# Writing out PE's four loops in a hybrid decoder step (GLA, short convolution, PEER experts)

## What is computed

```python
h = rmsnorm(x, norm1_g)
p = h @ w_in                                   # 2048 -> 16400
q, k, v, r, alr, cb, cc, cx, ga, gb = split(p)
loga = log_sigmoid(alr @ w_alpha_up + b_alpha) / 16
o, s_gla_new = gla_chunked(q, k, v, loga, s_gla)       # 4 heads, 256 x 512 states
y_a = silu(r) * rmsnorm(o, gla_norm_g)
u = cc * cx;  z = conv_b + sum_j buf[:, j:j+L] * conv_w[j]   # width 3
y_b = cb * z
m = sigmoid(ga) * y_a + sigmoid(gb) * y_b
x = x + m @ w_out
x = x + peer(rmsnorm(x, norm2_g), w_query, sub_keys, expert_u, expert_v)
y = rmsnorm(x, norm_f_g)
```

## Time and profile before

| what | value |
|---|---|
| median of 3 runs | 2507.85 us (2504.65 to 2508.5) |
| the profiled execution | 2509.17 us, of which its span is 2506.9 us |
| mean granted TensorE clock | 0.856 |
| PE busy | 1855.8 us (74%), 9451 matmuls |
| DVE busy | 1654.6 us (66%) |
| POOL busy | 967.6 us (39%) |
| ACT busy | 633.3 us (25%) |
| PE busy from 255 to 417 us (first head) | 160.92 of 162 us |
| PE busy from 601 to 767 us (third head) | 165.11 of 166 us |
| DMA share from 1240 to 2507 us (experts) | 1.00, 416 GB/s |

### The profile page before, as it was taken

The page is one execution under the profiler, slowest core; times in us unless marked ns, Lnnn a source line. Parts: engine busy times, 40 slices in busy tenths (PEclk is TensorE's granted clock), DMA queues, the critical chain, the costliest instruction groups (busy, mean ns, idle before and its releaser), DMA issues.

```text
span 2506.9 us, 26095 instructions
## 1 busy us (share of the span) xinstructions
PE 1855.8 (74%) x9451; PEld 1298.4 (52%) x9451; DVE 1654.6 (66%) x2086; ACT 633.3 (25%) x876; POOL 967.6 (39%) x761
## 2 busy tenths in 40 slices
PE   7999999999999998863655665665555456666564
PEld 6999888889888888852323332322212122122221
DVE  4444454545545545467687887788988887678776
ACT  5433554544545543321110011100101010010000
POOL 0000211111111100024476665666766656567653
PEclk9999999999999999976787887877787767976777
DMA  6665776776776766448899999999999999999997
GB/s 176 174 176 155 222 219 197 219 207 190 224 205 202 224 189 178 123 152 310 335 424 413 414 415 414 426 427 426 410 426 426 427 426 427 426 414 413 426 427 316
DMA packets 424229, 777.17 MB, mean 310 GB/s; under 512 B 14040, under 2 KB 344144, under 8 KB 355464
## 3 DMA queue, kind: packets, MB, share of 16 engines
q0 software_dynamic: 89168, 597.86, 57.8%
q1 hardware_dynamic: 333792, 175.71, 25.5%
q10 hardware_dynamic: 1168, 2.18, 0.2%
HBM read 754.51 MB, written 21.25 MB: 309 GB/s over the span
## 4 chain that ended last, share of the span: by engine, by line
DMA 29%; PE 15%; POOL 7%; DVE 6%; issue 3%; another core or an unknown queue 1%; ACT 1%; ACTq 0%; DVEq 0%; SPq 0%; POOLq 0%
DMA ring<-in_expert_v,idx_all 21%; PE bank L1643 8%; POOL ring L635 7%; DMA raw<-in_w_query 3%; DMA ring<-in_expert_u,idx_all 3%; DVE ring L1294 2%; PE bank L1489 2%; PE bank L1490 1%; PE bank L1491 1%; DVE x_tok L1312 1%; DMA ring<-in_expert_v,idx_s 1%; PE bank L1632 1%; PE bank L1633 1%; PE bank L1634 1%
## 5 line engine op out<-in xcount | busy, mean ns | idle before, releaser
L1643 PE MATMUL bank<-ring,diag 128*128 128x512 f32 x1000 | 672.7, 835 | 497.9 <-DMA ring<-in_expert_v,idx_all 421.4
L1643 PEld LDWEIGHTS bank<-ring,diag 128*128 128x128 f32 x1000 | 260.2, 273 | 899.4 <-issue 816.2
L1294 DVE CUSTOM_DVE_ANT_0 ring<-ring,xn_tok 128x2048 f32<-128x2048 f32 x256 | 583.4, 2289 | 200.1 <-DMA ring<-in_expert_u,idx_all 196.5
L1489 PE MATMUL bank<-act_hi,w_hi 128*128 128x264 f32 x2352 | 686.1, 292 | 17.7 <-DVE act_lo L1157 8.0
L1490 PE MATMUL bank<-act_lo,w_hi 128*128 128x264 f32 x2352 | 673.0, 286 | 0.0
L1491 PE MATMUL bank<-act_hi,w_lo 128*128 128x264 f32 x2352 | 672.0, 286 | 0.0
L964 DVE TENSOR_TENSOR w_lo<-raw,w_hi 128x2048 fp32r<-128x2048 f32 x147 | 337.0, 2292 | 428.6 <-ACT w_hi L665 428.3
L635 POOL DMA_INDIRECT ring<-in_expert_u,idx_all x256 | 443.0, 1730 | 265.4 <-DVE w_all L1294 131.6
L635 POOL DMA_INDIRECT ring<-in_expert_v,idx_all x256 | 391.0, 1527 | 256.8 <-PE bank L1643 182.6
L1489 PEld LDWEIGHTS bank<-act_hi,w_hi 128*128 128x128 f32 x2352 | 449.2, 191 | 76.9 <-issue 68.5
L665 ACT ACTIVATE w_hi<-raw 128x2048 fp32r<-128x2048 f32 x161 | 307.8, 1913 | 648.0 <-PE bank L1491 497.7
(11 more groups left out here) (231 smaller groups left out, 1321.3 us busy)
## 6 DMA issues: line engine op xcount, KB each, us to landing
raw<-in_w_in SPq DMA_DIRECT2D x129, 1024.0 KB, 6.3
s_ring<-in_state_gla POOLq DMA_DIRECT2D x64, 256.0 KB, 5.3
out<-s_ring POOLq DMA_DIRECT2D x64, 256.0 KB, 5.5
raw<-in_w_out SPq DMA_DIRECT2D x16, 1024.0 KB, 5.9
raw<-in_w_query SPq DMA_DIRECT2D x16, 1024.0 KB, 34.3
v_row<-v_samples POOLq DMA_DIRECT2D x32, 256.0 KB, 5.0
ring<-in_expert_u,idx_all POOLq DMA_INDIRECT x256, 14.0
ring<-in_expert_v,idx_all POOLq DMA_INDIRECT x256, 14.7
```

The lines of the kernel that those rows point to most:

```text
L1294: v.tensor_tensor_reduce(ring[k][:], ring[k][:], xn_tok[:, b // PH, :], 1.0, 0.0, ALU.mult, ALU.add, w_all[:, b * TOPK + s:b * TOPK + s + ...
L1489: mm(out, hi_, act_hi[:, k, :], start=(k == 0), stop=False)
L1643: ins = mm(bank[sum_bank(t) + j][:], diag[nth % N_DIAG][:], ring[k][:, j * 512:(j + 1) * 512], start=first, stop=final)
```

## The change

PE's four loops become Python loops, so that each turn is written out in the program with constants for its waits. The computation, the order of PE's matmuls and the semaphores stay. SP, ACT, DVE and POOL keep their loops.

```diff
             for b in range(1, 4):
                 project(B_Q + b)
-            with pe.Fori(0, 3) as i:
+            for i in range(3):
                 for b in range(4):
                     project(B_Q + 4 + b, i, 4)
             pe.wait_ge(la_ev, H * KD)
             project(B_V)
-            with pe.Fori(0, 3) as i:
+            for i in range(3):
                 for b in range(4):
                     project(B_V + b + 1, i, 4)
                     to_tokens(B_V + b, i, 4)
...
-            with pe.Fori(0, H) as i:
+            for i in range(H):
                 for b in range(SIX_PER_HEAD):
                     head_step(i, b)
             project(B_OUT, parts_from=KT)
-            with pe.Fori(0, 3) as i:
+            for i in range(3):
                 for b in range(4):
                     project(B_OUT + b + 1, i, 4)
                     to_tokens(B_OUT + b, i, 4)
```

## The result

| | before | after |
|---|---|---|
| median on the same chip | 2506.25 us (2504.13 to 2508.5, 4 runs) | 2486.08 us (2482.5 to 2492.09, 4 runs) |
| ratio | | 0.9925, 95% interval 0.9911 to 0.9938 |
| the profiled execution, its span | 2509.17 us, 2506.9 us | 2482.5 us, 2481.0 us |
| first matmul of block 144 (L1489), the last of the output projection | 1050.24 us | 1035.15 us |
| from there to the end of the span | 1456.7 us | 1445.8 us |

The kernel became 20.2 us faster in the median. The prediction was 13.2 us faster, with a range that ended at 2490 us, so the result lies outside it. In the two traces 15.1 us of the difference lie before block 144, where the change is, and 10.8 us behind it, where the program is the same.

A forecast was written before the change was run, and what follows sets the result against it. No engine bounds the whole span: PE until about 1060 us, then full DMA queues. Gains 8.52 + 5.62 less 0.9 gave 13.2 us, from the median 2507.85 to 2494.6 us; range 2490 to 2502.5 us.

The forecast's parts named there:

- Term 1: PE's instruction-fetch stalls at the head loop's three back branches vanish when written out: 8.52 us gained.
- Term 2: PE's half clock in block 0 after each of the three stalls goes with them: 5.62 us gained.
- Term 3: At the first head change ACT is late, w_lo follows, and PE waits before block 2: 0.9 us lost, once.
- Term 4: Back branches of the q and k, v and output projection loops are already free: zero gain.
- Term 5: Small loops written out need nine to ten more instruction packets, fetched without a stall: cost zero.
- the 75 to 82: Sign expected in the profile after: queue q8 carries 75 to 82 instruction packets instead of 72.
- the last sentence of the sum: After the heads, the rest, with a DMA-bound expert part of fixed work, moves forward unchanged.
- given back later: Expert part: w_query loads fall differently against gathers after the shift, 5 us either way, 2490 to 2500 us; chance 0.13.
- The rivals on the slow side: Straight-line fetches stall in the small stages, 2.9 us per new packet, 29 us in all: 2523.6 us; chance 0.04.

The follow-up runs named there:

- e1: Only PE's head loop written out, the three small loops kept, against the kernel before: 2488.86 us, ratio 0.994.
- e2: Only PE's three small loops written out, the head loop kept, against the kernel before: 2518.34 us, ratio 1.0047.
- e10: e2 with 16 semaphore increments ahead of PE's first wait, shifting its later instructions: 2502.54 us, ratio 0.9994 to the kernel before.
- e8: The changed kernel run once more, unaltered: 2485.41 us, ratio 0.9918 to the kernel before.
- e11: The changed kernel with second-half raw_lo and query later in each expert block and soft_exp between ACT's copies: 2483.28 us, ratio 0.991 to the kernel before.
- e7: The kernel before run once more, unaltered: 2504.17 us, ratio 0.9996.
- e5: The kernel before with 14 late w_query loads as whole rows (8 KB pieces, not 512 B), computing other numbers: 2474.26 us, ratio 0.9878.
- e6: The changed kernel with the 14 late w_query loads as whole rows, computing other numbers: 2460.94 us, ratio 0.9823 to the kernel before.
- e12: The kernel before with second-half raw_lo and query later in each expert block and soft_exp between ACT's copies: 2500.46 us, ratio 0.9977.
- e3: The kernel before with 128 semaphore increments ahead of PE's first wait: 2510.15 us, ratio 1.0021.

## Why the prediction was wrong, step by step

**Term 1, the stalls (8.52 us): right.** The distances are 0.31 to 0.32 us, and e1 alone has the projections' gain. That it is the fetch at a back branch is shown by e2 and e10, where only the position of the code changes the stall, and by q8: in the kernel before it carries one packet between 417.6 and 418.5 us, right behind L1599 at 417.44, and none from there to the matmul at 420.63.

**Term 2, the low clock (5.62 us): right.** The granted clock is 1.00 behind the head changes. Measured as what fell away between the starts of blocks 56 and 58, 80 and 82, and 104 and 106, the three places gave 4.27, 5.77 and 4.13 us, together 14.2, against 8.52 + 5.62 = 14.14.

**Term 3, what is late next (0.9 us): right in place and nearly in size.** ACT in the changed kernel at the first head change:

```profile
418.88 3.29 ACTq L840 DMA_DIRECT2D out<-u_rows  x1
...
422.80 0.42 ACTq L843 DMA_DIRECT2D out<-S  x1
423.72 1.28 ACT L665 ACT_TABLE_LOAD   x1 [5.00 <-PE bank L1491]
```

The table load comes at 423.72 instead of 416.86 + 6.17 = 423.03, and PE waited 0.6 us for DVE, 1.2 in e8 and 1.1 in e11. ACT's first issue took 3.29 us instead of 3.60, and from the end of its last issue (423.22) to the table load it is 0.5 us, where the sum had estimated 0.4. It is not named in the prediction that L1553's waits would shrink from 2.0 to 1.1 us, which gave 0.9 back. Block 0 was 0.7 us shorter in this trace (7.5 us instead of 8.1, and 0.1 us earlier), which makes up the rest of the 15.1 us before block 144. In e7 and e8 the same distance is 13.6 us.

**Term 4, the small loops (zero): right**, by e10 and e1. What I had not seen is that writing them out moves the head loop's target; the change as a whole is safe from it, since it has no back branch left.

**Term 5, more fetches (zero): right.** 75 packets, at the lower end of the 75 to 82. The extra ones of the small stages are nearly offset by those that a turn of the head loop fetched twice (65 packets in e1, 82 in e2).

**The step that failed** is the last sentence of the sum, that the expert part has fixed work and "moves forward as it is", and with it the price of the rival "given back later", 5 us either way as a sixth of one load, with 0.13. The sum had nothing for this part. Of the 20.2 us between the medians about 14 are the projections', as predicted, and about 6 lie here; between e7 and e8 it is 5 to 6 again, and in the first pair of traces 10.8, part of which is luck of the draw. What carries it is DVE's wait for `w_query` at L1214, as the table and e5 with e6 show. Why it is shorter in the changed kernel in the median too stays open; e12 and e11, whose traces have no such wait, still differ by 17.2 us in their medians. The earlier trace rows already held a 33 us load in the chain; the view in which it shows its price, DVE's waits between 1060 and 1300 us with 18.7 us at L1214, I had not read for this. It can be 5.8 to 19.1 us from trace to trace, and the trace before had nearly the worst of it. A range down to 2507.85 - 13.2 - 0.9 x 13 = 2483 us would have held the median; the draws of e1, e7 and e8 are of that size. The rivals on the slow side were not seen in the changed kernel, though e2 shows that the small stages' code can cost 14 us, by another mechanism than the one I named.

## What to carry to other kernels

In this kernel a hardware loop whose body does not stay resident cost PE 2.6 to 3.1 us at each branch back, plus 1.4 to 2.7 us of low clock, and 3.3 to 4.0 us more where its target seems to lie just before the end of an instruction packet; look for "issue" waits at the loop's first instruction, and read the entry to the loop as the control. The loops that stay resident gained nothing by being written out. Before a shift is taken to pass unchanged through a later stage, look for in-order waits there whose length depends on two DMA streams meeting, and put their whole size into the range.

## What the runs showed of the hardware that I had not expected

- The same head loop costs 11 us more when 16 instructions fewer stand ahead of it (block 144 at 1062.75 us in e2, at 1051.69 in e10; the medians are 15.8 us apart, on two chips): a second stall of 3.3 to 4.0 us behind each of three back branches.
- The 14 late `w_query` loads of 1 MB, most of them between gathers of 8 KB pieces, take 39.8 us in the median and up to 62.6 in 512 B pieces, and 9.0 us (6.6 to 10.4) in 8 KB pieces; the medians shown with e5 include the two early loads. The expert part is 34 us shorter with it (1456.7 to 1422.5 us).
- ACT's first DMA issue at L840 takes 3.60 us before, 3.29 after, 3.84 in e7 and 3.87 in e8, the three later ones 0.24 to 0.26.
- 128 semaphore increments at the start of PE's program took 19.4 us (e3, 0.15 us each) and delayed block 0 by 4.1 us; 16 of them (e10) were over at 3.5 us and did not delay it.
